# The MLP of blocks 1 to 3 as seven half-size products instead of eight, in a streaming encoder step

## The reference

```python
z = rmsnorm(h, norm_mix) @ w_in            # pool input 512 | q 512 | k 128 | v 128 | pool gate 1024 | attention gate 1024
h = h + (sigmoid(gp) * pool_out(z) + sigmoid(ga) * (attention(z) @ w_attn_up)) @ w_out
h = h + square(relu(rmsnorm(h, norm_mlp) @ w_up)) @ w_down     # w_up 1024 x 4096, w_down 4096 x 1024
y = rmsnorm(h, norm_final)
```

## Time and profile before

| | |
|---|---|
| median of 3 runs | 2447.85 us (2447.26 to 2447.87) |
| span of the profiled execution, first to last instruction | 2446.3 us |
| TensorE matmuls busy | 2423.0 us, 12933 instructions |
| TensorE weight loads busy | 2055.9 us |
| VectorE busy | 1328.5 us |
| ScalarE busy | 789.8 us |
| GpSimd busy | 173.1 us |
| moved by DMA | 237.20 MB, mean 97 GB/s |
| granted TensorE clock, mean | 0.997 of full |

### The profile page before, as it was taken

The page is one execution under the profiler, slowest core; times in us unless marked ns, Lnnn a source line. Parts: engine busy times, 40 slices in busy tenths (PEclk is TensorE's granted clock), DMA queues, the critical chain, the costliest instruction groups (busy, mean ns, idle before and its releaser), DMA issues.

```text
span 2446.3 us, 32439 instructions
## 1 busy us (share of the span) xinstructions
PE 2423.0 (99%) x12933; PEld 2055.9 (84%) x12933; DVE 1328.5 (54%) x1712; ACT 789.8 (32%) x1258; POOL 173.1 (7%) x168
## 2 busy tenths in 40 slices
PE   8999999999999999999999999999999999999997
PEld 8999999999977888888887788888887788888885
DVE  7645644445675564543576556445467555544444
ACT  4533322222443332222335334222243434222222
POOL 1400000000131000000024000000003400000000
PEclk9999999999999999999999999999999999999998
DMA  4223332222232333333332233332334233333231
GB/s 164 75 77 99 118 92 87 86 86 88 90 126 71 105 127 95 95 94 94 95 129 75 84 109 125 94 95 93 94 94 131 63 94 103 95 95 94 94 94 61
DMA packets 72248, 237.20 MB, mean 97 GB/s; under 512 B 8784, under 2 KB 9136, under 8 KB 72144
## 3 DMA queue, kind: packets, MB, share of 16 engines
q1 hardware_dynamic: 67408, 227.00, 30.0%
q10 hardware_dynamic: 4736, 8.75, 0.9%
HBM read 226.97 MB, written 8.85 MB: 96 GB/s over the span
## 4 chain that ended last, share of the span: by engine, by line
PE 99%; DVE 0%; DMA 0%; ACT 0%; DVEq 0%; issue 0%; SPq 0%; ACTq 0%
PE prod L335 95%; PE auxB L335 1%; PE auxA L439 1%; PE auxB L470 1%; PE auxB L453 1%; PE auxA L335 0%; DVE hT L774 0%; DMA raw<-weights 0%; DVE acc L756 0%; PE auxA L409 0%; DVE wL L728 0%; ACT wH L527 0%; DVE nL L762 0%; DVE acc L750 0%; DVE hT L944 0%; ACT acc L554 0%
## 5 line engine op out<-in xcount | busy, mean ns | idle before, releaser
L527 ACT ACTIVATE wH<-raw 128x1024 fp32r<-128x1024 f32 (+1 forms) x424 | 439.4, 1036 | 1530.3 <-PE prod L335 1526.7
L335 PE MATMUL prod<-nH,wH 128*128 128x512 f32 (+1 forms) x2320 | 747.1, 355 | 8.2 <-DVE nL L762 8.2
L335 PE MATMUL prod<-nL,wH 128*128 128x512 f32 (+1 forms) x2320 | 741.6, 352 | 0.0
L335 PE MATMUL prod<-nH,wL 128*128 128x512 f32 (+1 forms) x2320 | 741.4, 352 | 0.0
L728 DVE TENSOR_TENSOR wL<-raw,wH 128x1024 fp32r<-128x1024 f32 (+1 forms) x424 | 520.2, 1227 | 96.7 <-ACT wH L527 96.0
L335 PE MATMUL prod<-midL,wH 128*128 128x512 f32 (+1 forms) x1600 | 511.1, 352 | 0.0
L335 PE MATMUL prod<-midH,wL 128*128 128x512 f32 (+1 forms) x1600 | 511.1, 352 | 0.0
L335 PE MATMUL prod<-midH,wH 128*128 128x512 f32 (+1 forms) x1600 | 510.9, 352 | 0.0
L335 PEld LDWEIGHTS prod<-nH,wH 128*128 128x128 f32 x2320 | 407.9, 188 | 76.6 <-DVE wL L728 8.4
L335 PEld LDWEIGHTS prod<-nL,wH 128*128 128x128 f32 x2320 | 407.8, 188 | 61.2 <-issue 1.2
L335 PEld LDWEIGHTS prod<-nH,wL 128*128 128x128 f32 x2320 | 406.5, 188 | 60.6
(11 more groups left out here) (118 smaller groups left out, 1352.1 us busy)
## 6 DMA issues: line engine op xcount, KB each, us to landing
raw<-weights SPq DMA_DIRECT2D x392, 512.0 KB, 3.5
raw<-weights SPq DMA_DIRECT2D x32, 320.0 KB, 2.9
xT<-x SPq DMA_DIRECT2D x3, 2048.0 KB, 8.2
y<-hT ACTq DMA_DIRECT2D x12, 512.0 KB, 2.8
xT<-x SPq DMA_DIRECT2D x8, 272.0 KB, 5.3
y<-hT ACTq DMA_DIRECT2D x4, 544.0 KB, 2.8
rope<-tables SPq DMA_DIRECT2D x4, 512.0 KB, 4.4
cst<-consts SPq DMA_DIRECT2D x1, 96.0 KB, 6.6
```

What stands on the lines that cost most here:

```text
L335: ins = nc.tensor.matmul(out[:, s, 0:hi - lo], lhs, rhs[:, lo:hi], start=first, stop=last)
L527: return nc.scalar.activation(out, in_, ACT.Copy, scale=scale)
```

## The change

Block 0's MLP stays as it is but for the order of its tiles (ORD) and the second square of the hidden tile, which moves from VectorE to ScalarE. In blocks 1 to 3 each phase (up or down of one quarter: a 1024 x 1024 weight matrix by 512 columns) is cut 2 x 2 x 2 and done by one level of Strassen's method in Winograd's form: 7 products of quarter matrices (512 x 512 weights by 256 columns) in place of 8. Each of the 7 is made for 4 tiles of 128 features ("pairs" j = 0 to 3), so a phase has 28 products, called tokens, in the order ORDER; a token has 4 contraction tiles x 3 matmuls of 256 columns. Three of the 7 use a quarter of the weights as it is, four use a sum of quarters. The sums are made by GpSimd in block 0 from the units that are loaded there anyway, stored to DRAM (`weight_sums`, 32 sets of 1 MB) and loaded in blocks 1 to 3 like other weights. Each token's 128 x 512 weight is split to high and low when it comes: ScalarE 8 tokens ahead, VectorE 7 ahead, into a ring of 8. The data needs sums too: T1 to T4 of the normed input (`gain_pair`) and of the hidden layer (`sum_T13`, `sum_T2`, `sum_T4`), made by VectorE, with 7 high and 7 low parts per pair. The up products are gathered in PSUM and in a buffer z; the down products are added to hT one by one. The loops over quarters are written out, and SBUF is laid out by hand.

```diff
+ORDER = [(0, 1), (0, 5), (1, 1), (1, 5), (0, 2), (1, 2), (0, 6), (0, 3), (1, 6), (1, 3), (0, 7), (1, 7), (2, 5), (0, 4),
+         (2, 2), (1, 4), (2, 1), (3, 5), (3, 1), (3, 2), (2, 6), (2, 3), (3, 6), (3, 3), (2, 7), (3, 7), (2, 4), (3, 4)]
+NT7 = len(ORDER)
+TOKENS = PHASES * NT7
+RING = 8
...
+            def store_sums(p):
+                wait(sp, s_S, p)
+                sp.dma_start(sums_d[p], wsum[p % 2][:, :, :]).then_inc(set_out[p % 2], 16)
...
+            def token(b, ph, k, kps):
...
+                        if r == 5 and j >= 2:
+                            wait(pe, s_t1, b, q, j - 2)
...
+                        if r in (6, 3, 7, 4):
+                            wait(pe, {6: s_z1, 3: s_z2, 7: s_z0, 4: s_t2}[r], b, q, j)
...
+                for kp in kps:
...
+                    if down and k in (0, 4):
+                        wait(pe, s_L5 if k == 0 else s_L2, b, q, kp)
...
+                    nc.tensor.matmul(out, wh, xh, start=kp == 0 and r in (1, 2, 5), stop=False, skip_group_check=True)
+                    nc.tensor.matmul(out, wh, xl, start=False, stop=False, skip_group_check=True)
+                    ins = nc.tensor.matmul(out, wl, xh, start=False, stop=kp == PAIRS - 1, skip_group_check=True)
...
+            def phase(b, ph):
+                every = (0, 1, 2, 3)
+                if ph % 2:
+                    for k in range(6):
+                        token(b, ph, k, (0, 1))
+                    for k in range(6):
+                        token(b, ph, k, (2, 3))
...
# ScalarE
+            def copy_p1(b, q, j):
+                if j >= 2:
+                    wait(act, s_L2, b, q, j - 2)
...
+                copy(z(j, 1, 2), bank_a(j).unsqueeze(1)).then_inc(s_z1.sem, 1)
...
+            def high5(b, q, j):
+                wait(act, s_T2, b, q, j)
...
+                copy(m7H[:, 0:5, j, :], z(j, 1, 6)).then_inc(s_H5.sem, 1)
+
+            def high2(b, q, j):
+                wait(act, s_T4, b, q, j)
+                copy(m7H[:, 5:7, j, :], z(j, 6, 8)).then_inc(s_H2.sem, 1)
...
+                if k == 18:
+                    copy_p1(b, q, 2)
+                    copy_p5(b, q, 2)
...
+                weights_ahead(b, 2 * q * NT7 + k)
+                if q == 0 and k == 6:
+                    root("h", b)
...
+                if k == 17:
+                    high2(b, q, 1)
...
# VectorE
+            def gain_pair(b, m):
+
+                j, pos = m % PAIRS, ORD.index(m)
+                wait(dve, s_g, b, m)
...
+                tt(z(j, 7, 8), z(j, 6, 7), z(j, 5, 6), ALU.add).then_inc(s_gT4.sem, 1)
+                add_square("h", b, pos)
+                wait(dve, s_gH5, b, j)
+                low(n7L[:, 2:7, j, :], z(j, 3, 8), n7H[:, 2:7, j, :]).then_inc(s_gL5.sem, 1)
...
+                if kind == "out" and b > 0:
+                    gain_pair(b, m)
+                if b > 0 and i + 1 == M_MLP:
+                    for t in raw_tokens(b, 4, RING):
+                        split_low_token(b, t)
...
+            def up_step(b, q, k):
+                if q == 0 and k == 6:
+                    invert("h", b)
+                    wait(dve, s_r, "h", b)
+                if k == 7:
+                    add_cb(b, q, 0)
+                    weights_ahead(b, 2 * q * NT7 + k)
+                    relu_z01(b, q, 0)
+                    return
...
+                if k in (10, 11):
+                    add_u3(b, q, k - 10)
+                    weights_ahead(b, 2 * q * NT7 + k)
+                    relu_z2(b, q, k - 10)
+                    return
...
+                if k == 13:
+                    relu_z3(b, q, 0)
+                    sum_T13(b, q, 1)
+                    weights_ahead(b, 2 * q * NT7 + k)
+                    sum_T2(b, q, 1)
+                    return
+                if k == 14:
+                    low5(b, q, 0)
+                if k == 15:
+                    relu_z3(b, q, 1)
+                    sum_T4(b, q, 0)
+                if k == 16:
+                    low2(b, q, 0)
+                if k == 17:
+                    low5(b, q, 1)
+                    sum_T4(b, q, 1)
+                if k == 18:
+                    low2(b, q, 1)
...
+                if k == 27:
+                    sum_T13(b, q, 3)
+                    relu_z3(b, q, 3)
+                    sum_T2(b, q, 3)
+                    low5(b, q, 2)
+                    sum_T4(b, q, 2)
+                    low5(b, q, 3)
+                    sum_T4(b, q, 3)
+                    low2(b, q, 2)
+                    low2(b, q, 3)
+                weights_ahead(b, 2 * q * NT7 + k)
...
+            def down_step(b, q, k):
+                j, r = ORDER[k]
+                if r != 2:
+                    add_product(b, q, j, r)
+                weights_ahead(b, (2 * q + 1) * NT7 + k)
...
+                    if k == 1:
+                        invert("x", b + 1)
+                    if k % 2 == 0 and 2 <= k <= 2 * KD:
+                        gained_low("x", b + 1, k // 2 - 1)
...
# GpSimd, after the mixer of block 0
+            def sum_weights(p):
...
+                link(tt(s[:, 2, :], a11, a21, ALU.subtract))
+                link(tt(s[:, 1, :], s[:, 2, :], a22, ALU.subtract))
+                tt(s[:, 0, :], s[:, 1, :], a11, ALU.subtract)
+                tt(s[:, 3, :], a12, s[:, 1, :], ALU.add).then_inc(s_S.sem, 1)
```

More of the change, by code:

```diff
@@ L243, in wait_product @@
-        def wait_product(eng, b, i):
[L245 to L261, removed]
+        splits = []
+        for b in blocks:
+            splits += [("mix", b, i) for i in range(M_MLP)]
+            if b == 0:
+                splits += [("plain", 0, n) for n in range(2 * KD * NQ)]
+            else:
+                splits += [("tok", b, t) for t in range(TOKENS)]
@@ L308, in _ @@
             sp.dma_start(v_old_out, vold).then_inc(copy_out, 16)
[L310 to L324, removed]
+            for i in range(RAW, M_MLP):
+                load_mixer_unit(0, i)
+                if i == ROPE_LOAD:
+                    load_rope(1)
+            for n in range(2 * KD * NQ):
+                load_plain_unit(n)
+                if n == 3:
+                    wait(sp, s_h, 0, KD - 1)
+                    sp.dma_start(xT[:, :, 0:TB], x123[0, :, :, :]).then_inc(x_in, 16)
+                if n % 2 and n >= 7:
+                    store_sums((n - 7) // 2)
@@ L336, in stream, with three @@
                 return ins
-            def three(out, b, uslot, off, high, low, k, first, last):
-                wh, wl = wH[:, uslot, off:off + P], wL[:, uslot, off:off + P]
+            def three(out, b, wslot, off, high, low, k, first, last):
+                wh, wl = wslot[:, 0, off:off + P], wslot[:, 1, off:off + P]
                 stream(out, b, wh, high[:, k, :], first, False)
@@ L389, in before @@
                         sum_squares("f", b - 1)
-                product(b, i % 2, high, low, nk, before)
+                product(b, i, high, low, nk, before)
             def sum_squares(kind, b):
@@ L519, in _ @@
                     between(b, i)
-                quarters(pe, b, up, down, lambda b: down(b, NQ - 1))
+                if b == 0:
+                    for q in range(NQ):
+                        plain_up(q)
+                        plain_down(q)
+                else:
+                    for ph in range(PHASES):
+                        phase(b, ph)
             sum_squares("f", NB - 1)
@@ new lines, in plain_down @@
+            def plain_down(q):
+                for i in range(KD):
+                    n = 16 * q + KD + i
+                    wait_plain(act, n)
+                    plain_split_ahead(n + 2)
+                    if q == NQ - 1:
+                        m = ORD[i]
+                        gained_high("x", 1, i)
+                        if i == 0:
+                            root("x", 1)
+                        act.wait_ge(down_added, hid(q, i))
+                        square("f", 0, i, hT)
+                        wait(act, s_sq, "f", 0, i)
+                        copy(hT[:, m, :], hT[:, m, :], g_fin[:, m:m + 1]).then_inc(s_fg.sem, 1)
@@ new lines, in plain_up @@
+            def plain_up(q):
+                for i in range(KD):
+                    m, n = ORD[i], 16 * q + i
+                    wait_plain(dve, n)
+                    if n == 0:
+                        plain_split_ahead(n + 2)
+                        wait(dve, s_r, "h", 0)
+                    y = work[:, i % 2, :]
+                    stt(out=sview(y, 0), in0=pview(prod[i % 2], 0), scalar=0.0, in1=sview(rms, 0),
+                        op0=ALU.max, op1=ALU.mult).then_inc(relu_done, 1)
+                    if n > 0:
+                        plain_split_ahead(n + 2)
+                    dve.wait_ge(hid_sq, hid(q, i))
+                    low(midL[:, m, :], y, midH[:, m, :]).then_inc(hid_low, 1)
+                    if q == 0 and i >= 4:
+                        add_square("x", 1, 2 * i - 8)
+                        add_square("x", 1, 2 * i - 7)
```

840 lines of the change are left out of this document (638 added, 202 removed).

## The result

The changed kernel takes **2496.99 us** (median of 4 runs, 2495.01 to 2498.49) against 2447.86: a ratio of 1.020 (95% interval 1.0187 to 1.0212), 2.0% slower where 2387 us was forecast. The first fence has lines of the page of the kernel after, against the earlier trace rows: busy time, the busy tenths of TensorE in 40 slices, the chain that ended last by line, and DMA issues (KB, us to landing).

The account below looks back on a forecast made before the run. TensorE's matmul issue was taken to bound the kernel. A gain of 117 us from fewer columns, less 56 us of stalls (26 + 18 + 9 + 3), left 61 us: 2387 us forecast, range 2370 to 2405.

Parts of the forecast that it names:

- block 0's: Block 0's MLP: GpSimd's sums and the 32 stores are covered, costing 0 to 4 us in all at up-to-down turns.
- (d): Rival, half-size products: a fresh tile every 256 columns costs the whole 188 ns load record, 2895 us; chance 0.06 with near misses.
- Pace: Blocks 1 to 3, half-size products: 8064 matmuls of 256 columns at 118.0 ns each, 951.6 us, replacing 1068.6 us.
- The line: Matmul price drawn through 272 and 512 columns: 4.1 ns plus 0.445 ns per column, 118.0 ns at 256.
- N/2.4 + 2.5: The Trainium skill's matmul issue estimate: 109.2 ns at 256 columns, a gain of 188 us; the forecast set it aside.
- First phase of a block: Blocks 1 to 3: late splits 2.0 us, token 13's wait 2.3, later stall 1.7 more; 6.0 x 3 = 18 us.
- Token 20 and turn to down: Each up phase: 1.4 us wait before token 20, then 0.5 and 0.3 at its end; 2.2 x 12 = 26 us.
- Last down phase: Blocks 1 and 2: waits of 2.6 us at token 10, 1.4 at 11, 0.3 at 9; 4.3 x 2 = 9 us.
- GpSimd beside VectorE: Block 0's MLP: VectorE's splits slow beside GpSimd, but +2.1 us per product is covered except at the up-to-down turns.
- Transfers: Weight loads at 185 GB/s against 90 to 95 before: a load is late by about 1 us at most.
- (a): Rival: the stalls vanish, hand sum too pessimistic; with 20 us left, 2351 us; chance 0.17.
- (c): Rival: VectorE operations cost their full recorded times, 4.5 us of stalls a phase instead of 2.2; 2414 us; chance 0.13.

Follow-up runs that it names:

- e1: Changed kernel with SP issuing the store of each weight-sum set two loads earlier: 2420.57 us, ratio 0.989 to the kernel before.
- e12: e9 plus ScalarE splitting the weight of the product after next before waiting for h and gain_pair in out products: 2376.92 us, ratio 0.971.
- e3: GpSimd's sums, their stores and waits left out, summed tokens loading plain weight quarters (result incomplete, one execution): 2421.36 us.
- e7: e1 plus an earlier P1 copy of pair 2 on ScalarE, and two of each four hand-over splits put behind the pair's gain: 2398.35 us.
- e5: Half-size products stream 128 columns per matmul instead of 256, half the output left out, other work kept (one execution): 3197.39 us.
- e9: e7 plus earlier sum of squares, root and reciprocal, and gained_low in steps 8 to 22 of the last down phase: 2392.66 us.

## Why the prediction was wrong, by its own steps
**The step that failed** is block 0's: "a pair of units has 12.0 us and needs at most 4 x 1.76 = 7.1, so the loads that wait for the sum keep some 2 products of margin", and "32 stores of 1 MB in block 0 add 85 GB/s: no cost". Both look at work and rate. The sums do take 5.8 us and the stores' rate does cost nothing, but the queue has an order, and a store (8.2 us to land, a latency that the forecast never put in) stood between two sums. 0 to 4 us were forecast, 78 came, and all but 1 of them go when the ring is cut: block 1's MLP starts at 966.8 us in the kernel after and at 889.2 in e1, 885.2 before, and 3.4 of the 4 us that are left are the out products'. (The whole kernel gains 76: e1's first phase in block 1 is 1.5 us longer.) No rival had it. The slower rival, (d), was about weight loads; a pace of 120.0 ns with a load for each matmul refutes it.

The other terms, the 34 us between the forecast 2387 and e1's 2420.6:
- *Pace*: 118.0 forecast, 120.0 measured, 8064 x 2.0 = 16 us. The line was drawn outside its two points. The quoted N/2.4 + 2.5 would have been 11 ns off, more than the rows were. That each tile serves two matmuls in a row in block 0 was misread: every matmul there has its own load.
- *Out products*: no term at all; 44.6 became 48.0 us, 3 x 3.4 = 10. The forecast counted what `gain_pair` adds, only from the last product on, and missed that ScalarE's weight split had moved behind it (e12: 15.7 us with what follows).
- *First phase of a block*: 52.7 us. Above 40.3 of matmuls and 0.9 for the sum of squares (there before too) that is 11.5, with the turn to down behind it 12.1; forecast were 8.2. Token 4 starts 5.1 us late, where 2.0 were forecast: the wait of 2.2 us inside the first token was not foreseen. Up to token 13 another 3.4 us come (0.8 and 2.4 of waits behind the reciprocal), 2.3 forecast. From there to token 21 it is 3.0, against 1.4 + 1.7 forecast, as said. 3 x 3.9 = 12.
- *Token 20 and turn to down*, the nine other pairs of phases: 1.3 and 0.6 us, in the place and, for token 20, by the chain that were named; 1.4 and 0.8 forecast. 9 x 0.27 = 2.4 us too much.
- *Last down phase*: 4.3 forecast, 4.1 measured. The sum is right in part by luck: 2.6, 1.4 and 0.3 us were forecast before tokens 10, 11 and 9, and it is 0.9, 1.3, 1.3 and 0.3 before tokens 8, 10, 11 and 16.
- *GpSimd beside VectorE*: covered, as said (e3). *Transfers*: at 179 GB/s in the MLP no load was late enough to show; as said. Of the 3 us set aside for block 0 and the hand-overs some 2 were not used.

16 + 10 + 12 - 2.4 - 0.4 - 2 = 33 of 34. The mechanism of the forecast for blocks 1 to 3, gain given back to waits made by the order of ScalarE and VectorE, was right, its size too small: 8064 matmuls at 120.0 ns leave 101 us, of which the kernel after gives back 72 in blocks 1 to 3 (56 of 117 were forecast). It can be undone in part: e12 has 71 us of the 101. Rivals (a) and (c) fall: the stalls of an ordinary pair of phases neither vanish by themselves nor grow to 4.5 us.

## What to carry to other kernels
Follow every buffer that is given back by a transfer around its whole ring: who writes it, which queue entry sends it off, what stands ahead of that entry, and how long it takes to land; two buffers are worth one if the transfer of the first is queued behind the second's producer. Where an engine gets a new wait at the head of a step, ask what else in that step was early before. A hand-run schedule with rows' durations found the waits of an ordinary pair of phases (2.2 us forecast, 1.9 measured) and of the last down phase (4.3 and 4.1); the misses lay in the stretches it was not run over: the out products, the first token behind them, and block 0's queue.

## What the runs showed of the hardware
- **The clock.** In the kernel after the granted clock falls to half in ten short stretches of block 0, where TensorE stood for up to 2.9 us every 15 us (mean 0.97 over block 0's window above; 1.00 in e1, without those waits), and again in the blocks' first phases. There it costs nothing as long as waits for other engines follow. The first phases of blocks 1, 2 and 3 of e7 are 49.5 us long each, at three granted clocks:

```profile
889.20:938.70 49.50, 42.79 (x339) 40.97 (x339) 44.26 (x73) 34.49 (x66) 0.00 (x0) 1.00 0.69 212
1466.90:1516.40 49.50, 43.86 (x339) 42.37 (x339) 44.26 (x73) 34.47 (x66) 0.00 (x0) 0.97 0.69 212
2044.50:2094.00 49.50, 45.07 (x339) 43.96 (x339) 44.26 (x73) 34.63 (x66) 0.00 (x0) 0.93 0.55 170
```

TensorE is busy 1.1 and 2.3 us longer in blocks 2 and 3 and waits that much less for the other engines, which set the pace there (one wait for VectorE is 1.1 us in block 3 and 1.8 in the others). So the stretches that e7's expectation hoped to win back were worth nothing there. Where one came behind the last wait of such a phase, in block 1 of e1, the phase is 1.5 us longer (54.2 against 52.7). In e5 the clock fell within 1.5 us of the end of a pause of 2.5 us in the first token and stayed at half for 577 to 594 us of nearly unbroken matmuls of 128 columns. Halving the columns of every matmul made that kernel 700 us slower.
- **A store's landing.** 1 MB took 8.0 us from issue (the median of 32) behind two loads of 512 KB, where 512 KB loads land in 3.5; in e1 and e9, where the store does not close a ring, the median is 6.6.
- **GpSimd and VectorE.** One GpSimd operation of 512 elements took 1.29 us where it started first and 2.27 where it started during one of VectorE's two-input operations; VectorE's took longer in the same way (timelines of e1, first GpSimd's, then VectorE's):

```profile
506.61 1.29 POOL L1582 TENSOR_TENSOR wsum<-wsum,raw 128x512 f32<-128x512 f32 x1
507.86 2.27 POOL L1583 TENSOR_TENSOR wsum<-raw,wsum 128x512 f32<-128x512 f32 x1
```
```profile
506.63 2.35 DVE L1128 TENSOR_TENSOR wm<-raw,wm 128x1024 fp32r<-128x1024 f32 x1 [0.37 <-ACT wm L745]
508.91 1.81 DVE L1128 TENSOR_TENSOR midL<-work,midH 128x544 fp32r<-128x544 f32 x1
```

VectorE's split, 1.23 us alone, starts at 506.63 and ends 1.1 us behind the end of GpSimd's operation (507.90); GpSimd's next, 1.29 alone, ends 1.2 us behind the end of that split (508.98); VectorE's next, 0.73 alone, ends 0.6 us behind the end of GpSimd's (510.13). That is each waiting for the other's end in turn rather than both running slower, and agrees with what the Trainium skill (SBUF — State Buffer, SBUF: two separate sides) says of a pair of ports that the two share by an exclusive lock.
